# Modulation parts turned by transposes into a bank per slot and summed on VectorE, instead of products with a folding matrix

## The reference

```python
silu_c = jax.nn.silu(c)
for l in range(DEPTH):
    mod = silu_c @ p["w_mod"][l] + p["b_mod"][l]
    sh1, sc1, gt1, sh2, sc2, gt2 = jnp.split(mod[:, None, :], 6, axis=-1)
    h = rmsnorm(x, p["norm1_g"][l]) * (1.0 + sc1) + sh1
    mix, r_new, v_rows = token_mixing(h, pos, r0, p, l)
    x = x + gt1 * mix
    h = rmsnorm(x, p["norm2_g"][l]) * (1.0 + sc2) + sh2
    x = x + gt2 * hier_moe(h, p, l)
```

## Time and profile before

| | us |
|---|---|
| median of 3 runs | 1760.63 |
| lowest and highest | 1757.57, 1762.81 |
| the profiled execution, its own time | 1762.88 |
| its span, first to last instruction | 1761.3 |

### The profile page before, as it was taken

One profiled execution on the slowest core, in us unless ns is written; L12 is line 12 of the kernel. 1 busy time (PEld: TensorE's weight loads), 2 busy tenths in 40 slices (PEclk: granted clock), 3 DMA queues, 4 the chain that ended last, 5 costly groups with the idle time before them and its releaser, 6 DMA issues. The chain is left out here.

```text
span 1761.3 us, 20399 instructions
## 1 busy us (share of the span) xinstructions
PE 1689.8 (96%) x8346; PEld 979.0 (56%) x8346; DVE 526.7 (30%) x1265; ACT 257.5 (15%) x502; POOL 51.3 (3%) x101
## 2 busy tenths in 40 slices
PE   6999999999899999999999999999989998999997
PEld 3677754445477554444447777544536775444443
DVE  1220210124511343443442212102253116244446
ACT  3110001101110222111130100010112003211111
POOL 0000000000100100000000000000011010000000
PEclk9999999999999989999999999999999999999999
DMA  9623465377853548999983336434778333799994
GB/s 399 248 110 143 191 240 238 144 287 302 309 201 143 199 167 356 421 420 421 423 344 127 128 122 268 155 144 189 289 310 311 125 115 144 275 421 421 422 420 168
DMA packets 47022, 451.69 MB, mean 256 GB/s; under 512 B 5633, under 2 KB 5889, under 8 KB 7505
## 3 DMA queue, kind: packets, MB, share of 16 engines
q1 hardware_dynamic: 43200, 409.65, 58.7%
q10 hardware_dynamic: 2304, 33.56, 4.5%
q0 software_dynamic: 1424, 7.16, 1.0%
HBM read 411.16 MB, written 39.19 MB: 256 GB/s over the span
## 5 line engine op out<-in xcount | busy, mean ns | idle before, releaser
L658 PE MATMUL ps<-ring,work 128*64 128x512 f32 x1536 | 341.5, 599 | 2.7 <-ACT work L1052 2.7
L658 PE MATMUL ps<-ring,hT 128*32 128x128 f32 (+1 forms) x1920 | 318.6, 382 | 2.5 <-DMA ring<-stream 2.1
L658 PE MATMUL ps<-hT,ring 128*128 128x288 f32 x1280 | 317.8, 410 | 1.9 <-DVE work L1598 1.9
L658 PEld LDWEIGHTS ps<-hT,ring 128*128 128x128 f32 x1280 | 244.4, 192 | 72.8 <-issue 6.1
L658 PE MATMUL ps<-work,ring 128*128 128x288 f32 x1024 | 249.6, 406 | 4.1 <-issue 2.3
L658 PEld LDWEIGHTS ps<-ring,hT 128*32 128x32 f32 (+1 forms) x1920 | 154.4, 137 | 167.5 <-issue 163.4
L1052 ACT ACTIVATE work<-ps 128x512 f32<-128x512 f32 (+5 forms) x244 | 109.6, 469 | 849.6 <-PE ps L658 848.9
L658 PEld LDWEIGHTS ps<-ring,work 128*64 128x64 f32 x1536 | 114.0, 138 | 212.3 <-issue 209.1
L658 PEld LDWEIGHTS ps<-work,ring 128*128 128x128 f32 x1024 | 194.2, 190 | 58.7 <-issue 5.4
L658 PE MATMUL ps<-work 128*128 128x288 f32 (+6 forms) x800 | 189.5, 399 | 5.8 <-DVE hT L1741 2.6
L658 PEld LDWEIGHTS ps<-work 128*128 128x128 f32 (+2 forms) x800 | 125.3, 187 | 68.6 <-issue 36.5
(11 more groups left out here) (178 smaller groups left out, 832.2 us busy)
## 6 DMA issues: line engine op xcount, KB each, us to landing
ring<-stream SPq DMA_DIRECT2D x96, 2048.0 KB, 8.7
ring<-stream SPq DMA_DIRECT2D x192, 1024.0 KB, 10.1
state_sample_out<-ring ACTq DMA_DIRECT2D x16, 2048.0 KB, 10.6
state_out<-prm POOLq DMA_DIRECT2D x8, 512.0 KB, 13.5
prm<-params SPq DMA_DIRECT2D x1, 2608.5 KB, 25.6
prm<-params POOLq DMA_DIRECT2D x1, 2608.5 KB, 15.6
cst<-consts SPq DMA_DIRECT2D x1, 1649.0 KB, 18.4
xT<-x_in SPq DMA_DIRECT2D x1, 1152.0 KB, 5.9
```

The lines of the kernel that those rows point to most:

```text
L658: return nc.tensor.matmul(out, lhsT, rhs, start=start, stop=stop, **k)
```

## The change

The product with `modfold` becomes a transpose of each 128 x 128 piece, which only turns it: a slot's four transposes fill a whole bank of 512 columns. The sum over the four parts moves to VectorE, as a `tensor_reduce` of 4 x 9 x 4 numbers per partition out of the bank (stride 32), followed by the addition of the bias. Each slot has a tile `modt` of its own, dealt with the others by turn (bank 7 for the last slot before `fold next` and `fold gate`, banks 3 and 4 for slots 4 and 5 of layer 1), and is taken on its own: at VectorE's next modulation step or at the step `fold`. Where TensorE issues a fold is unchanged.

```diff
+turn, waiting = 0, None
+
+
+def use_fold(b=None):
+    global turn, waiting
+    if waiting is not None:
+        use((*waiting, "modt"), turn % 7 if b is None else b)
+        turn += b is None
+    waiting = None
...
-        for _g in (g for g, group in GROUPS_OF_MODS.items() if _s == ("mod", group[0])):
-            use((_g, "modt"), YBANK)
         for _t in tiles_of(_s, _l):
             use((_l, _s, _t), turn % 7)
             turn += 1
+        if _s[0] == "mod" or _s[0] == "fold" and waiting is not None and FOLD_OF[waiting[1][1]][0:2] == (_l, _s[1]):
+            use_fold(YBANK if _s in (("fold", "next"), ("fold", "gate")) else None)
+        if _s[0] == "mod":
+            waiting = (_l, _s)
...
-            if LAST_MODS[_l]:
-                use(((_l, "last"), "modt"), 3)
+            for _n, _s in enumerate(LAST_MODS[_l]):
+                use((_l, _s, "modt"), 3 + _n)
...
                 l, step = pending.pop()
-                gl, name, n = FOLD_OF[step[1]]
-                key = ((gl, name), "modt")
-                wait_reads(pe, [(l, step, "modp")], free=key if n == 0 else None)
+                key = (l, step, "modt")
+                out = wait_free(pe, key, [(l, step, "modp")])
                 buf = modp[:, MOD_TURN[step[1]] % 2, :]
                 for c in range(4):
-                    at = (4 * n + c) * ROWS
-                    last = mm(ps[bank(key)][:, at:at + ROWS], buf[:, c * P:c * P + P], C("modfold"), True, True)
-                if n == len(GROUPS_OF_MODS[gl, name]) - 1:
-                    made(last, key)
+                    last = transposed(out[:, c * P:c * P + P], buf[:, c * P:c * P + P], C("ident"))
+                made(last, key)
...
-            def take_mods(group):
-
-                l, first = GROUPS_OF_MODS[group][0]
-                n = 4 * len(GROUPS_OF_MODS[group])
-                bias = (R("bmod") if l == 0 else bias_next)[:, 4 * first:4 * first + n].rearrange("p (f o) -> p f o", o=1).broadcast_to([P, n, ROWS])
-                out = wait_made(dve, (group, "modt"))
-                taken(dve.tensor_tensor(mod_of(l)[:, 4 * first:4 * first + n, :], cut(out[:, 0:n * ROWS], n, ROWS), bias, ALU.add), (group, "modt"))
+            waiting = []
+
+            def take_mod(group=None):
+
+                if not waiting or group is not None and FOLD_OF[waiting[0][1][1]][0:2] != group:
+                    return
+                key = (*waiting.pop(), "modt")
+                l, i = key[1][1]
+                bias = (R("bmod") if l == 0 else bias_next)[:, 4 * i:4 * i + 4].rearrange("p (f o) -> p f o", o=1).broadcast_to([P, 4, ROWS])
+                dst = mod_of(l)[:, 4 * i:4 * i + 4, :]
+                parts = wait_made(dve, key)[:, :].rearrange("p (c j r) -> p c r j", c=4, j=4)[:, :, 0:ROWS, :]
+                taken(dve.tensor_reduce(dst, parts, op=ALU.add, axis=AX.X), key)
+                settle()
+                dve.tensor_tensor(dst, dst, bias, ALU.add)
                 settle()
...
-                    if kind == "fold":
-                        if step == ("fold", "start"):
+                    if kind == "mod":
+                        if l == 0 and step == ("mod", (0, 0)):
                             dve.wait_ge(head_loaded, 48)
-                        take_mods((l, i))
+                        take_mod()
+                        waiting.append((l, step))
+                    elif kind == "fold":
+                        take_mod((l, i))
...
-                                take_mods((l - 1, "last"))
+                                for last in LAST_MODS[l - 1]:
+                                    waiting.append((l - 1, last))
+                                    take_mod()
```

More of the change, by code:

```diff
@@ L133, in use @@
     used[b] += 1
-turn = 0
+turn, waiting = 0, None
[5 more added lines that the diff above has]
+    waiting = None
 for _l in range(DEPTH):
```

## The result

| | before | after |
|---|---|---|
| median of the runs | 1761.22 us (4 runs, 1757.57 to 1762.81) | 1744.5 us (4 runs, 1740.33 to 1747.7) |
| profiled execution | 1762.88 us, span 1761.3, clock 0.981 | 1744.13 us, span 1742.6, clock 0.987 |
| PE busy | | 1669.2 us, 96%, 8250 matmuls |

The ratio is 0.991, interval 0.9891 to 0.9929: the change gains 16.7 us, 12.5 to 19.2 by the interval. The sign was right, the size was not.

A forecast was written before the change was run, and what follows sets the result against it. TensorE, busy 96% of the span, was taken to bound the kernel. Gains of 2.9 + 0.6 + 0.8 + 0.7 + 2.2 + 1.9 = 9.1 us off the median 1760.63 gave 1751.5 us, range 1745.5 to 1757.5.

The forecast's parts named there:

- A fold in dense work: Single folds among q, k, vr matmuls: each 0.48 us shorter; six in layer 0 (2.9 us), four in layer 1 (1.9 us).
- Slots 10 and 11: Two folds back to back in layer 0: 0.6 us gained, since slot 11 then waits for ScalarE's copy.
- Start of layer 0: Slots 0 to 3: gain 0, because token mixing waits 2.09 us for the DMA of its weights.
- Waits that only grow: Layer 0's route stage, layer 1's slots 0 and 1: gain 0, TensorE's waits of 2.51 and 1.71 us get longer.
- The bank order: Gather before pair 0: moved bank turns remove TensorE's waits of 0.62 us (layer 0) and 1.69 us (layer 1).
- No wait for the sums: TensorE never waits for a bank whose sum on VectorE is late, gather's g5 included: price 0.
- The sum: All places together: 2.9 + 0.6 + 0.8 + 0.7 + 2.2 + 1.9 = 9.1 us gained.
- rival 2: The clock takes it back: added 3.5 us half-clock stretches cost 1.7 us each; three give 1756.6 us; chance 0.20.
- slot 2: Layer 1's slot 2, folded at half clock before the gather in layer 0's route stage: 0.8 us gained.
- Rival 1: Folds gain, bank order does not, another reader being late at pair 0: 7.2 us in all, 1753.4 us; chance 0.17.
- Rival 3: Half-clock stretches follow each transposed slot in dense work: ten places, 17 us against 9.1, 1768.5 us; chance 0.05.
- Rival 4: New transposes come out as two instructions each: folds gain nothing, bank order 2.3 us, 1758.3 us; chance 0.03.

The follow-up runs named there:

- the run with this part alone: The kernel before with only the bank turns of its tiles moved as the change moves them, folding products kept: 1760.7 us, ratio 1.0007.
- the run with only the other part: The change with its transposes and sums, but every slot in the eighth bank and no tile moved: 1748.0 us, ratio 0.9935.
- the repeat: The kernel after, run again without any edit beside the kernel before: 1744.0 us, ratio 0.9918.

## Why the prediction was right or wrong

- **TensorE bounds the kernel, VectorE's work is nearly free.** Right: twice as many sums again, some 18 us on VectorE (48 of 0.38 us with the drain), cost 1.6 us.
- **A fold in dense work, 0.48 us less.** Right: 0.50 us from product to product. Ten places give 5.0 us, where the sum had 4.8.
- **Slots 10 and 11, 0.6 us less.** 0.5 us.
- **Start of layer 0, no gain.** 0.4 us, and the reason named was wrong: the wait there is on ScalarE and, through it, on VectorE. In a second execution of the unchanged kernel it is so too (1.53 us), so the wait for DMA was a feature of the one execution that the rows came from, not of the kernel.
- **Waits that only grow.** Right: 2.51 became 2.91 us, and 1.71 became 1.75 (the text had 2.2 for the latter).
- **The bank order, 0.5 us or so in layer 0 and 2.2 in layer 1.** Right: the waits of 0.62 and 1.69 us are gone, ScalarE's windows are late next in layer 0 by 0.20 us, and the run with this part alone gives 2.0 us at equal clock, the run with only the other part 2.7 less.
- **No wait for the sums.** One: 0.26 us at bank g5 of layer 0's gather, the bank named, since slot 2's sum came at 623.42 behind VectorE's clearing of buffers. It is on a weight load beside running matmuls and moved nothing that can be seen.
- **The sum.** 9.1 us forecast; at equal clock 1728.1 to 1729.2 became 1718.7, some 10 us.

**The step that failed is the clock.** The sum carried it at zero, and the text weighed it only against the change: rival 2 let 3.5 us stretches be added and spoke of one that "might as well fall away", 1.7 us, and the low end of the range held two of them. In the profiled pair 21.6 us of half-clock time fell away, 10.8 us; over all runs some 10 us, 5 us. The price of a stretch was right, the count was not. With the clock slot 2 was mis-sized too: its 0.8 us assumed that fold at half clock on both sides, and in the kernel after the clock is back at 615.3, before that fold. Chance had a part in the size: one kernel's own runs range over 20 us of half-clock time (45.5 to 66.9 in 24 runs of the kernel before), and the profiled pair's 10.8 us overstate the mean. At the ratio of the repeat, 0.9918, the 1761.22 us of the result would have become 1746.8, just above the low end of the range. That the gain exceeds the 9.1 us is beyond chance, since 1751.5 lies outside both intervals.

The place that lost most half-clock time is the one the rows showed: the 13.6 us at 0.50 in which the placing, a product and slot 2's nine-column fold lie, now 6.8.

Rival 1 falls: both waits are gone. Rival 2 has the wrong sign. Rival 3 falls: no stretch at half clock stands behind a dense transposed slot, and five times as many transposes gave the highest clock of all, 0.993. Rival 4 falls by the count of 96.

**What stays open.** That 128 columns raise the clock and 9 don't is shown by a pair of kernels with equal work time; the fold's bank and the sums on VectorE changed along with them in that pair, and neither is known to matter, as bank 7 for all slots left 50.1 us and three times the sums 50.0. Why columns count is not shown: both forms take 0.9 to 1.0 us a slot and look equally busy in the profile. Nor is it shown how they act on stretches far from any fold, as at 106 and 661. A rival is that some of these stretches hang on when a stage comes rather than on what stands in it. Against it, the kernels with transposes keep 45 to 51 us although their stages come at different times, but no run was made that only delays a stage. Nor is it shown why transposes, 48.5 us, come out between narrow products (58 to 63) and full ones (37.9); that they last half as long as the latter, and that five times as many give more clock, would fit, but a run with each slot transposed twice was not made.

## What to carry to other kernels

- Profile the unchanged kernel more than once before a term rests on who came last in a wait: here the second profile had another engine there.
- Keep two accounts of a change: work and waits at equal clock, and time at 1.2 GHz, half of which is lost. Forecast each by itself, and don't set the second to zero because its sign is unknown: where the change alters the work next to a stretch at half clock, put that whole stretch into the range, on both sides.
- Count a matmul by what it streams as well as by what it takes. Nine-column products cost as much time as 128-column ones here (0.91 against 0.99 us a slot) and left TensorE longer at 1.2 GHz.
- A wait of 2 to 3 us in thin work is worth filling with matmuls that nobody reads, sized to the wait: 6.8 us of filler gave 5 us, 13.7 us of it nothing.

## What the runs showed of the hardware

- A float32 product of 128x128 by 9 columns takes nearly as long as one by 128: 8 instructions in 0.91 and 0.99 us. A float32 transpose of 128x128 is one instruction of 0.11 us (20 in 2.24 us); the product with the identity is two.
- 384 more transposes in the folds' places lowered half-clock time from 48.5 to 24.7 us. As filler in layer 1, in place of matmuls of twice their time, they left a wait of 2.14 us and 6.8 us at half clock behind it, though the mean over the runs stayed at 51.1 us.
- The sum of 128x144 from PSUM to 128x36, strided, takes 0.31 us, as long as the plain addition that read the same 144 numbers.
- Repeats of one kernel differ in their granted clock (0.981 to 0.987 in 24 runs of the kernel before), and its medians in five groups run from 1759.1 to 1762.8 us. Much of the spread of a kernel's times is clock, so work at equal clock is the finer measure: 1728.1 to 1729.2 in these groups, though the two groups of 4 and 6 runs of the kernel after lie 2.2 us apart.
